# Raw key products kept in memory for the second half of a two-direction delta rule

## The chip, the cores and the metric

The kernel runs on one core of a Trainium2 chip. The metric is device time in microseconds (us) for one execution. The core has five instruction streams that run in order and meet only through semaphores: TensorE (PE in the profile; PEld is its weight load), VectorE (DVE), ScalarE (ACT), GpSimd (POOL) and SyncE (SP), which here issues DMAs.

## The reference, cut to what matters

The whole is one layer of an encoder: a projection, two mixers side by side, an output projection and a mixture of experts. The change lies in one of the mixers, a gated delta rule over 1024 tokens with 4 heads of 128, run forward and backward over the same keys, queries and values and summed:

```python
decay = where(tril, exp(g_i - g_j), 0)                 # g: cumulative log-decay, one per direction
a_mat = where(strict, einsum('id,jd->ij', k * beta, k) * decay, 0)
attn  = where(tril,   einsum('id,jd->ij', q, k) * decay, 0)
...
o_f = gated_delta_chunked(q, k, v, g[:, 0], beta[:, 0])
o_b = flip(gated_delta_chunked(flip(q), flip(k), flip(v), flip(g[:, 1]), flip(beta[:, 1])))
```

Per chunk `a_mat` (its system is inverted) and `attn` start from two raw products, keys by keys and keys by queries. These raw products don't depend on the direction; beta, decay and the mask do.

## The kernel before, in words

The function `delta_net` holds both directions, d = 0 and d = 1. A chunk is 128 tokens, so there are TT = 8 steps t; direction 0 takes chunk t in step t and direction 1 takes chunk 7 - t. Over the first four steps the two directions thus cover all eight chunks, and in the last four each meets the chunks that the other has already had.

There is one order of work, written out by hand in `delta_schedule` as a list of names with a step; every engine walks that same list and picks out the names it serves, for d = 0 and then d = 1. An engine never runs ahead of its own order. One round of the list (the loop variable t) mixes work of four steps: it starts with `z4` of step t and ends with `d6` of t; `read_k`, `read_q`, `solve`, `attend`, `new_state` belong to step t - 1, `kq` to t + 1 and `kk` to t + 2. Names that the prediction uses:

- `kk`: PE multiplies the keys of a chunk by themselves, 4 heads into the PSUM bank `O[d]`. DVE then makes `amat` of it (L1037): four `scalar_tensor_tensor` of 128x128, product times -beta times decay.
- `kq`: PE multiplies keys by queries into bank `V[d]`; DVE multiplies the bank by the masked decay into `attn` (L1046), one `tensor_tensor` of 128x512.
- `z4`, `d4`, `turn4`, `z5`, `d5`, `turn5`, `z6`, `d6`: the inverse of a chunk's system, built by doubling blocks. `z4` needs the 16-wide diagonal inverses spread out in memory by POOL (`spread_tt`, `spread_t`, L1150) and the masked level of `amat` (`alev4`, `alev5`, L1144, POOL). After `d4`, DVE adds (L1051) and PE transposes the sum (`turn4`, L936).
- `base`: DVE inverts the 16x16 diagonal blocks in small instructions (L996 to L1020), between the add of `d4` and that of `d5`.
- `read_k`: PE, keys by state; DVE makes the residual `resid` of it (L1061). `attend`: PE; when it is done POOL may write the next `mask` (L1157). `new_state`: PE, then DVE updates the state (L1075).
- `add_o`: only in steps 4 to 7, POOL adds an output to the sum (L1177).

POOL's order within a round is `alev4`, `vb` (L1163), `mask`, `alev5`, from step 4 on `add_o`, `spread_tt`, `spread_t`, two instructions of each (d = 0, 1). SP's queue stores `amat`, loads its diagonal blocks back, stores the inverses and loads them as `T_cols`.

A line with an "L910" is any product of the helper `heads`: it stands for all matmuls of 4 heads, told apart by their tiles. One such product for both directions shows as x16.

Of the kernel before, what the change touches and what calls it, by code (L numbers as in the profile page):

```python
# [26 lines left out]
ALU = mybir.AluOpType  # L27
ACT = mybir.ActivationFunctionType
AX = mybir.AxisListType

P = 128
# [3 lines left out]
TT = L // P  # L35
H = 4
# [738 lines left out]
def delta_net(nc, core, c, a, out, tb, o_sum, a_dram, x_dram, g_dram):  # L775
# [6 lines left out]
    qT, kT, kv = out["qT"], out["kT"], out["kv"]  # L782

    def buf(name, n=1):
        return [core.sb(f"{name}{d}", [P, n, H, P]) for d in range(2)]

    e_b, ab_b, as_b, at_b, tt_b = buf("decay", 2), buf("amat", 2), buf("alev", 2), buf("attn", 2), buf("TT", 2)
# [7 lines left out]
    inv_t = core.sb("blocks_inv_t", [NB, 256])  # L795
    prod = core.sb("blocks_prod", [NB, 512])
    half = core.sb("blocks_half", [NB, 64])
    X = [core.ps(f"bank_x{d}", [P, H, P]) for d in range(2)]
    Y = [core.ps(f"bank_y{d}", [P, H, P]) for d in range(2)]
    V = [core.ps(f"bank_v{d}", [P, H, P]) for d in range(2)]  # L800
    O = [core.ps(f"bank_o{d}", [P, H, P]) for d in range(2)]
    names = ("kk kq absd decay masked amat attn alev t16 tt16 z zc dd tt t tt6 ks r solved vn vdec vb qs o_part "
             "av kv o o_added state a_out blk_ld tc_ld t_out").split()
    S = {n: [core.sem(f"dn_{n}{d}") for d in range(2)] for n in names}
    gb_ld = [[core.sem(f"dn_gb_ld{d}{s}") for s in range(2)] for d in range(2)]
    based, base_step, x_out = core.sem("dn_based"), core.sem("dn_base_step"), core.sem("dn_x_out")
# [1 line left out]
    def chunk(t, d):  # L808
        return t if d == 0 else TT - 1 - t
# [23 lines left out]
    def late(d):  # L833
        return HALF[1 - d]
# [7 lines left out]
    with nc.Block() as block:  # L842
# [59 lines left out]
        @block.tensor  # L902
        def _(pe):
            def wait(name, d, n):
                if n > 0:
                    pe.wait_ge(S[name][d], n)

            def heads(dst, lhs, rhs):
                for h in range(H):
                    mm = pe.matmul(dst[:, h, :], lhs(h), rhs(h), start=True, stop=True)  # L910
                return mm

            for name, t, d in delta_schedule():
                cs, b = cols(t, d), t % 2
                if name == "kk":
                    wait("state", d, t - 1)
                    wait("amat", d, t)
                    heads(O[d], lambda h: kT[:, h, cs], lambda h: kT[:, h, cs]).then_inc(S["kk"][d], 1)
                elif name == "kq":
                    wait("attn", d, t)  # L920
                    wait("o", d, t - 1)
                    heads(V[d], lambda h: kT[:, h, cs], lambda h: qT[:, h, cs]).then_inc(S["kq"][d], 1)
                elif name == "z4":
                    wait("zc", d, 3 * t)
                    wait("alev", d, 2 * t + 1)
                    wait("tt16", d, t + 1)
                    heads(X[d], lambda h: as_b[d][:, 0, h, :], lambda h: tt16_b[d][:, 0, h, :]).then_inc(S["z"][d], 1)
                elif name == "d4":
                    wait("zc", d, 3 * t + 1)
                    wait("tt6", d, t)  # L930
                    wait("t16", d, t + 1)
                    heads(Y[d], lambda h: t16_b[d][:, 0, h, :], lambda h: z_b[d][:, 0, h, :]).then_inc(S["dd"][d], 1)
                elif name in ("turn4", "turn5"):
                    wait("tt", d, 2 * t + (1 if name == "turn4" else 2))
                    for h in range(H):
                        mm = pe.transpose(X[d][:, h, :], tt_b[d][:, b, h, :], c["ident"][:])  # L936
                    mm.then_inc(S["t"][d], 1)
                elif name == "z5":
                    wait("alev", d, 2 * t + 2)
                    wait("t_out", d, 2 * t + 1)  # L940
                    heads(X[d], lambda h: as_b[d][:, 1, h, :], lambda h: tt_b[d][:, b, h, :]).then_inc(S["z"][d], 1)
                elif name == "d5":
                    wait("zc", d, 3 * t + 2)
                    heads(Y[d], lambda h: t_b[d][:, 0, h, :], lambda h: z_b[d][:, 0, h, :]).then_inc(S["dd"][d], 1)
                elif name == "z6":
                    wait("t_out", d, 2 * t + 2)
                    wait("amat", d, t + 1)
                    lo, up = late(d), early(d)
                    for h in range(H):
                        mm = pe.matmul(X[d][up, h, 0:64], ab_b[d][lo, b, h, up], tt_b[d][lo, b, h, lo],  # L950
                                       start=True, stop=True)
                    mm.then_inc(S["z"][d], 1)
                elif name == "d6":
                    wait("zc", d, 3 * t + 3)
                    up = early(d)
                    for h in range(H):
                        mm = pe.matmul(Y[d][up, h, 0:64], t_b[d][up, 0, h, up], z_b[d][up, 0, h, 0:64],
                                       start=True, stop=True)
                    mm.then_inc(S["dd"][d], 1)
                elif name == "read_k":  # L960
                    wait("state", d, t + 1)
                    wait("attn", d, min(t + 2, TT))
                    wait("o", d, t)
                    heads(V[d], lambda h: kT[:, h, cs], lambda h: s_b[d][:, 0, h, :]).then_inc(S["ks"][d], 1)
                elif name == "read_q":
                    wait("amat", d, min(t + 3, TT))
                    heads(O[d], lambda h: qT[:, h, cs], lambda h: s_b[d][:, 0, h, :]).then_inc(S["qs"][d], 1)
                elif name == "solve":
                    wait("tt6", d, t + 1)
                    wait("r", d, t + 1)  # L970
                    heads(V[d], lambda h: tt_b[d][:, b, h, :], lambda h: r_b[d][:, 0, h, :]).then_inc(S["solved"][d], 1)
                elif name == "attend":
                    wait("vdec", d, t + 1)
                    wait("vn", d, t + 1)
                    heads(V[d], lambda h: at_b[d][:, b, h, :], lambda h: vn_b[d][:, 0, h, :]).then_inc(S["av"][d], 1)
                elif name == "new_state":
                    wait("o_part", d, t + 1)
                    heads(O[d], lambda h: rows(0, t, d)[:, h, :], lambda h: vd_b[d][:, 0, h, :]
                          ).then_inc(S["kv"][d], 1)

        @block.vector
        def _(dve):
            def wait(name, d, n):
                if n > 0:
                    dve.wait_ge(S[name][d], n)
# [42 lines left out]
            for name, t, d in delta_schedule():  # L1028
                ch, b = chunk(t, d), t % 2
                if name == "kk":  # L1030
                    wait("kk", d, t + 1)
                    wait("decay", d, t + 1)
                    wait("z", d, 3 * (t - 1))
                    wait("alev", d, 2 * (t - 1))
                    wait("a_out", d, 16 * (t - 1))
                    for h in range(H):
                        ins = dve.scalar_tensor_tensor(out=ab_b[d][:, b, h, :], in0=O[d][:, h, :],  # L1037
                                                       scalar=head_col("nbeta", t, d, h), in1=e_b[d][:, b, h, :],
                                                       op0=ALU.mult, op1=ALU.mult)
                    ins.then_inc(S["amat"][d], 1)  # L1040
                elif name == "base":
                    invert_blocks(t)
                elif name == "kq":
                    wait("kq", d, t + 1)
                    wait("masked", d, t + 1)
                    dve.tensor_tensor(at_b[d][:, b], V[d][:], at_b[d][:, b], ALU.mult).then_inc(S["attn"][d], 1)  # L1046
                elif name == "d4":
                    wait("dd", d, 3 * t + 1)
                    wait("tt16", d, t + 1)
# [6 lines left out]
                elif name == "read_k":  # L1056
# [3 lines left out]
                    for h in range(H):  # L1060
                        ins = dve.scalar_tensor_tensor(out=r_b[d][:, 0, h, :], in0=V[d][:, h, :],  # L1061
                                                       scalar=head_col("nbetaG", t, d, h), in1=vb_b[d][:, 0, h, :],
                                                       op0=ALU.mult, op1=ALU.add)
# [7 lines left out]
                elif name == "new_state":  # L1071
                    wait("kv", d, t + 1)
                    wait("state", d, t + 1)
                    for h in range(H):
                        ins = dve.scalar_tensor_tensor(out=s_b[d][:, 0, h, :], in0=s_b[d][:, 0, h, :],  # L1075
                                                       scalar=head_col("eTot", t, d, h), in1=O[d][:, h, :],
                                                       op0=ALU.mult, op1=ALU.add)
# [3 lines left out]
        def _(act):  # L1081
            def wait(name, d, n):
                if n > 0:
                    act.wait_ge(S[name][d], n)

            for name, t, d in delta_schedule():
                b, up = t % 2, early(d)
                if name == "decay":
# [4 lines left out]
                    ins.then_inc(S["absd"][d], 1)  # L1093
                    wait("absd", d, t + 1)
                    act.activation(e_b[d][:, b], e_b[d][:, b], ACT.Exp, scale=-1.0).then_inc(S["decay"][d], 1)
                elif name in ("z4", "z5"):
                    n = 3 * t + (1 if name == "z4" else 2)
                    wait("z", d, n)
# [1749 lines left out]
```

## Time and profile before

| what | us |
|---|---|
| median of 3 runs (lowest, highest) | 1543.13 (1542.45, 1543.61) |
| the profiled execution's own time | 1542.74 |
| its span, first to last instruction | 1541.0 |
| delta rule's stretch in the span | about 321 to 560 |
| PE busy over the span | 1321.7 (86%) |
| DVE, ACT, POOL busy over the span | 1086.2, 828.5, 397.1 |

The rows further down are read from one profiled execution. Each timeline row gives start, duration, engine, line, operation, the tiles (output<-inputs), the shape and a count; in brackets the idle time of the engine before it and what ended it. Rows with a count above 1 are merged neighbours.

### The profile page before, as it was taken

The numbers are of one execution on the slowest core, as the hardware profiler recorded it, in microseconds if no ns is written. First come the engines' busy times: TensorE is split into PE (matmuls) and PEld (weight loads), VectorE is DVE, ScalarE is ACT, GpSimd is POOL, SyncE is SP. The second block draws the span as 40 slices with busy tenths as digits, with TensorE's granted clock in tenths as the row PEclk, the third lists the DMA queues.
The fourth block names the chain that finished last, engine by engine and source line by source line (L and its number), as shares of the span: only waits on it lengthen the run. The fifth ranks groups of instructions, "written<-read, shape, count | busy, mean of one in ns | idle before, by whom it ended". The sixth has DMA issues, their size and how long they took to land. (4 is left out here: it accounts for less than half of the span.)

```text
span 1541.0 us, 23093 instructions
## 1 busy us (share of the span) xinstructions
PE 1321.7 (86%) x7750; PEld 1130.7 (73%) x7750; DVE 1086.2 (70%) x1339; ACT 828.5 (54%) x1025; POOL 397.1 (26%) x378
## 2 busy tenths in 40 slices
PE   4999999936999958787994589999999999999930
PEld 4999887836999957645883478888888888888820
DVE  5884886654777568904225588888888888888818
ACT  7563444432656450034221377777787778787712
POOL 5110220015565645702210011211111221111113
PEclk9999999967999978998996599999999999999975
DMA  8264976012221137721113399999999999999727
GB/s 250 90 212 151 302 222 179 9 57 52 49 67 46 22 150 276 271 110 32 42 42 123 138 366 399 421 409 411 408 408 410 412 413 412 407 406 413 319 93 291
DMA packets 149680, 357.85 MB, mean 232 GB/s; under 512 B 41999, under 2 KB 94443, under 8 KB 122475
## 3 DMA queue, kind: packets, MB, share of 16 engines
q1 hardware_dynamic: 131803, 297.12, 51.5%
q0 software_dynamic: 11904, 40.42, 7.9%
q10 hardware_dynamic: 5904, 19.40, 3.1%
q8 instruction: 42, 0.69, 0.2%
q14 instruction: 27, 0.22, 0.0%
HBM read 287.62 MB, written 69.27 MB: 232 GB/s over the span
## 5 line engine op out<-in xcount | busy, mean ns | idle before, releaser
L2647 DVE TENSOR_TENSOR w_lo<-w_down,w_hi 128x2048 fp32r<-128x2048 f32 x66 | 148.4, 2288 | 65.7 <-ACT w_hi L2588 65.7
L2647 DVE TENSOR_TENSOR w_lo<-w_gate,w_hi 128x2048 fp32r<-128x2048 f32 x66 | 149.6, 2287 | 15.3 <-ACT w_hi L2588 15.3
L2588 ACT ACTIVATE w_hi<-w_up 128x2048 fp32r<-128x2048 f32 x66 | 126.7, 1923 | 49.9 <-PE down_mm L2541 49.9
L2647 DVE TENSOR_TENSOR w_lo<-w_up,w_hi 128x2048 fp32r<-128x2048 f32 x66 | 150.5, 2286 | 3.8 <-ACT w_hi L2588 0.2
L2479 POOL COPY gather_idx<-slot_token 128x1 int32 (+1 forms) x34 | 26.6, 781 | 486.0 <-PE x_turned L2503 453.5
L2588 ACT ACTIVATE w_hi<-w_down 128x2048 fp32r<-128x2048 f32 x66 | 123.4, 1914 | 45.8 <-issue 22.7
L2588 ACT ACTIVATE w_hi<-w_gate 128x2048 fp32r<-128x2048 f32 x66 | 126.8, 1923 | 30.3 <-PE up_mm L2515 29.5
L2513 PE MATMUL gate_mm<-w_hi,gathered_T_hi 128*128 128x512 f32 x264 | 107.5, 407 | 10.6 <-DVE w_lo L2647 5.3
L2539 PE MATMUL down_mm<-w_hi,hidden_T_hi 128*128 128x512 f32 x264 | 106.8, 404 | 9.0 <-DVE hidden_T_lo L2681 9.0
L2513 PE MATMUL up_mm<-w_hi,gathered_T_hi 128*128 128x512 f32 x264 | 105.9, 401 | 0.0
L2514 PE MATMUL gate_mm<-w_lo,gathered_T_hi 128*128 128x512 f32 x264 | 105.1, 398 | 0.0
L2515 PE MATMUL gate_mm<-w_hi,gathered_T_lo 128*128 128x512 f32 x264 | 104.9, 397 | 0.0
L2540 PE MATMUL down_mm<-w_lo,hidden_T_hi 128*128 128x512 f32 x264 | 103.9, 394 | 0.0
L2541 PE MATMUL down_mm<-w_hi,hidden_T_lo 128*128 128x512 f32 x264 | 103.8, 393 | 0.0
L2515 PE MATMUL up_mm<-w_hi,gathered_T_lo 128*128 128x512 f32 x264 | 103.3, 391 | 0.0
L2514 PE MATMUL up_mm<-w_lo,gathered_T_hi 128*128 128x512 f32 x264 | 102.8, 389 | 0.0
L2482 POOL DMA_INDIRECT gathered<-h_rows,gather_idx x34 | 81.9, 2410 | 26.9 <-POOL gather_idx L2479 26.9
L283 PE MATMUL proj_ps<-hT_hi,w_split 128*128 128x512 f32 x192 | 77.4, 403 | 0.0
L284 PE MATMUL proj_ps<-hT_lo,w_split 128*128 128x512 f32 x192 | 75.9, 395 | 0.0
L285 PE MATMUL proj_ps<-hT_hi,w_split 128*128 128x512 f32 x192 | 75.9, 395 | 0.0
L2513 PEld LDWEIGHTS gate_mm<-w_hi,gathered_T_hi 128*128 128x128 f32 x264 | 50.9, 193 | 28.0 <-issue 18.1
L2539 PEld LDWEIGHTS down_mm<-w_hi,hidden_T_hi 128*128 128x128 f32 x264 | 50.2, 190 | 18.7 <-DVE w_lo L2647 9.1
(430 smaller groups left out, 3359.9 us busy)
## 6 DMA issues: line engine op xcount, KB each, us to landing
w_down<-in_expert_w_down SPq DMA_DIRECT2D x66, 1024.0 KB, 6.9
w_gate<-in_expert_w_gate SPq DMA_DIRECT2D x64, 1024.0 KB, 7.6
w_up<-in_expert_w_up SPq DMA_DIRECT2D x64, 1024.0 KB, 8.3
expert_rows_dram<-expert_out ACTq DMA_DIRECT2D x33, 512.0 KB, 8.5
expert_rows_dram<-ones SPq DMA_DIRECT2D x32, 512.0 KB, 6.3
s_rows<-s_rows_dram SPq DMA_DIRECT2D x9, 1184.0 KB, 6.1
x<-s_rows_dram SPq DMA_DIRECT2D x7, 1184.0 KB, 5.2
w_raw<-in_w_in SPq DMA_DIRECT2D x12, 512.0 KB, 6.0
```

Of the source, the lines that this page charges most:

```text
L283: pe.matmul(dst, left(0), right(0), start=k == 0, stop=False)
L284: pe.matmul(dst, left(0), right(1), start=False, stop=False)
L285: return pe.matmul(dst, left(1), right(0), start=False, stop=k == KT - 1)
L2482: pool.indirect_dma_start(out=xg[:, s, :], out_offset=None, in_=h_dram, in_offset=bass.IndirectOffsetOnAxis(ap=idx[:, s:s + 1], axis=0)).t ...
L2513: pe.matmul(dst, xT_hi[:, k, :], hi[:, at, cols], start=k == 0, stop=False)
L2514: pe.matmul(dst, xT_hi[:, k, :], lo[:, at, cols], start=False, stop=False)
L2515: mm = pe.matmul(dst, xT_lo[:, k, :], hi[:, at, cols], start=False, stop=k == KT - 1)
L2539: pe.matmul(dst, hT_hi[:, k, :], hi[:, at, cols], start=k == 0, stop=False)
L2540: pe.matmul(dst, hT_hi[:, k, :], lo[:, at, cols], start=False, stop=False)
L2541: mm = pe.matmul(dst, hT_lo[:, k, :], hi[:, at, cols], start=False, stop=k == KD - 1)
L2588: act.activation(hi[:, slot(s, j), :], flat(j), ACT.Copy).then_inc(S["piece_hi"], 1)
L2647: dve.tensor_tensor(lo[:, at, :], flat(j), hi[:, at, :].bitcast(F32), ALU.subtract).then_inc(S["piece_lo"], 1)
```

## The change

Two buffers in SBUF, `k_keys` and `k_queries`, hold the raw products of all eight chunks. In steps 0 to 3 the PE makes the products as before, DVE uses them from PSUM as before, and ACT then copies the banks to the buffers, 16 copies in all; the PE's next use of the bank also waits for the copy. In steps 4 to 7 the PE makes neither product, and DVE reads the other direction's copy from SBUF.

```diff
+    k_keys = core.sb("keys_by_keys", [P, TT, H, P])
+    k_queries = core.sb("keys_by_queries", [P, TT, H, P])
+    SHARED = TT // 2
@@ PE
-                if name == "kk":
+                if name == "kk" and t < SHARED:
                     wait("state", d, t - 1)
                     wait("amat", d, t)
+                    wait("kept_kk", d, t)
                     heads(O[d], ...kT..., ...kT...).then_inc(S["kk"][d], 1)
-                elif name == "kq":
+                elif name == "kq" and t < SHARED:
                     wait("attn", d, t)
+                    wait("kept_kq", d, t)
                     wait("o", d, t - 1)
                     heads(V[d], ...kT..., ...qT...).then_inc(S["kq"][d], 1)
                 elif name == "read_k":
                     wait("state", d, t + 1)
-                    wait("attn", d, min(t + 2, TT))
+                    wait("attn", d, min(t + 2, SHARED))
+                    wait("kept_kq", d, min(t + 2, SHARED))
                 elif name == "read_q":
-                    wait("amat", d, min(t + 3, TT))
+                    wait("amat", d, min(t + 3, SHARED))
+                    wait("kept_kk", d, min(t + 3, SHARED))
@@ DVE
                 if name == "kk":
-                    wait("kk", d, t + 1)
+                    if t < SHARED:
+                        wait("kk", d, t + 1)
+                    else:
+                        wait("kept_kk", 1 - d, TT - t)
+                    gram = O[d] if t < SHARED else k_keys[:, ch]
                     ...
-                        ins = dve.scalar_tensor_tensor(..., in0=O[d][:, h, :],
+                        ins = dve.scalar_tensor_tensor(..., in0=gram[:, h, :],
                                   scalar=head_col("nbeta", t, d, h), in1=e_b[d][:, b, h, :],
                 elif name == "kq":
-                    wait("kq", d, t + 1)
+                    if t < SHARED:
+                        wait("kq", d, t + 1)
+                    else:
+                        wait("kept_kq", 1 - d, TT - t)
+                    gram = V[d][:] if t < SHARED else k_queries[:, ch]
                     wait("masked", d, t + 1)
-                    dve.tensor_tensor(at_b[d][:, b], V[d][:], at_b[d][:, b], ALU.mult)
+                    dve.tensor_tensor(at_b[d][:, b], gram, at_b[d][:, b], ALU.mult)
@@ ACT
+                elif name == "kk" and t < SHARED:
+                    wait("amat", d, t + 1)
+                    act.activation(k_keys[:, chunk(t, d)], O[d][:], ACT.Copy).then_inc(S["kept_kk"][d], 1)
+                elif name == "kq" and t < SHARED:
+                    wait("attn", d, t + 1)
+                    act.activation(k_queries[:, chunk(t, d)], V[d][:], ACT.Copy).then_inc(S["kept_kq"][d], 1)
```

## Rows read from the trace of the kernel before

**Rows 1.** One round by windows: length, busy us of each engine, granted clock, DMA

```profile
472.10:496.45 24.35, 24.16 (x225) 23.32 (x224) 18.05 (x54) 14.53 (x40) 14.45 (x13) 1.00 0.20 55
```

**Rows 2.** Timeline around z4 of step 5, PE

```profile
473.15 2.05 PE L910 MATMUL bank_o<-kT 128*128 128x128 f32 x16
...
475.04 1.95 PE L910 MATMUL bank_v<-qT,kT 128*128 128x128 f32 x16
...
477.81 2.05 PE L910 MATMUL bank_x<-TT,alev 128*128 128x128 f32 x16
...
483.60 1.27 PE L936 MATMUL bank_x<-ident,TT 128*128 128x128 f32 x8 [0.17 <-DVE TT L1051]
```

**Rows 3.** Timeline of the same stretch, DVE

```profile
471.26 2.16 DVE L1075 SCALAR_TENSOR_TENSOR state<-state,tab_eTot,bank_o 128x128 f32<-128x128 f32 x8 [1.08 <-PE bank_o L910]
474.35 2.16 DVE L1037 SCALAR_TENSOR_TENSOR amat<-bank_o,tab_nbeta,decay 128x128 f32<-128x128 f32 x8 [0.93 <-PE bank_o L910]
476.42 1.29 DVE L1046 TENSOR_TENSOR attn<-bank_v,attn 128x512 f32<-128x512 f32 x2
480.79 2.16 DVE L1061 SCALAR_TENSOR_TENSOR resid<-bank_v,tab_nbetaG,vb 128x128 f32<-128x128 f32 x8 [3.08 <-PE bank_v L910]
482.87 1.29 DVE L1051 TENSOR_TENSOR TT<-TT,bank_y 128x512 f32<-128x512 f32 x2
```

**Rows 4.** Timeline of the same stretch, POOL

```profile
468.71 1.28 POOL L1157 TENSOR_TENSOR attn<-decay,upto_f 128x512 f32<-128x512 f32 x1 [8.99 <-PE bank_v L910]
...
473.64 2.50 POOL L1150 TENSOR_TENSOR TT<-T_cols,diag 128x512 f32<-128x512 f32 x2
...
479.11 1.27 POOL L1144 TENSOR_TENSOR alev<-amat,level_f 128x512 f32<-128x512 f32 x1 [0.53 <-PE bank_x L910]
```

**Rows 5.** Timeline of a later round, POOL's add_o and PE's z4 of step 7

```profile
522.32 2.51 POOL L1177 TENSOR_TENSOR o_sum<-o_sum,otmp 128x512 f32<-128x512 f32 x2
...
526.20 3.26 PE L910 MATMUL bank_x<-TT,alev 128*128 128x128 f32 x16 [1.61 <-POOL TT L1150]
```

**Rows 6.** All instructions of two DVE lines: ns min/median/max, first and last start

```profile
L1046 DVE TENSOR_TENSOR attn<-bank_v,attn x16: 677/690/692, 336.7 to 523.7; 128x512 f32<-128x512 f32 x16
...
L1007 DVE TENSOR_TENSOR blocks_prod<-blocks_inv,blocks x8: 682/684/685, 342.2 to 513.3; 64x512 f32<-64x512 f32 x8
```

**Rows 7.** Timeline of the same small DVE instruction, beside POOL and alone

```profile
360.61 1.26 POOL L1157 TENSOR_TENSOR attn<-decay,upto_f 128x512 f32<-128x512 f32 x1
360.88 1.01 DVE L1000 TENSOR_TENSOR blocks_prod<-blocks_inv,blocks 64x8 f32<-64x8 f32 x1
...
387.57 0.16 DVE L1000 TENSOR_TENSOR blocks_prod<-blocks_inv,blocks 64x8 f32<-64x8 f32 x1
```

**Rows 8.** Timeline of a later stage, two neighbouring DVE instructions beside POOL

```profile
643.49 0.61 DVE L1870 TENSOR_TENSOR s_z<-s_rot 128x256 f32<-128x256 f32 x1
643.77 0.91 POOL L1903 TENSOR_TENSOR s_back<-s_scanned,s_rows 128x254 f32<-128x254 f32 x1
644.02 0.95 DVE L1871 TENSOR_TENSOR s_z<-s_rot 128x256 f32<-128x256 f32 x1
```

**Rows 9.** All instructions of a DVE line in the stage after this one

```profile
L1982 DVE TENSOR_TENSOR silu_z<-silu_z,gn_rs x8: 678/1752/1758, 568.8 to 578.6; 128x512 f32<-128x512 f32 x8
```

**Rows 10.** Windows after PE stood idle; the number behind POOL's is the clock

```profile
375.00:377.00 2.00, 2.00 (x11) 2.00 (x11) 0.23 (x1) 0.14 (x1) 1.01 (x1) 0.51 0.49 49
...
527.00:529.00 2.00, 1.94 (x10) 1.75 (x10) 0.00 (x0) 0.60 (x1) 2.00 (x3) 0.54 0.00 0
...
530.00:531.00 1.00, 1.00 (x8) 1.00 (x8) 0.01 (x1) 0.09 (x1) 0.00 (x0) 0.71 0.00 0
```

**Rows 11.** Timeline, ACT before and in z4 of step 5

```profile
477.63 0.78 ACT L1115 ACTIVATE TT<-bank_y 64x256 f32<-64x256 f32 x2 [4.00 <-PE bank_y L957]
479.00 0.60 ACT L1100 ACTIVATE zc<-bank_x 128x512 f32<-128x512 f32 x1 [0.60 <-PE bank_x L910]
```

**Rows 12.** Timeline, DVE in the first round and PE after its longest later idle time

```profile
337.95 0.69 DVE L1046 TENSOR_TENSOR attn<-bank_v,attn 128x512 f32<-128x512 f32 x1 [0.54 <-POOL attn L1157]
...
371.18 1.97 PE L936 MATMUL bank_x<-ident,TT 128*128 128x128 f32 x8 [7.75 <-DVE TT L1055]
```

More of the change, by code:

```diff
@@ L802, in delta_net @@
     names = ("kk kq absd decay masked amat attn alev t16 tt16 z zc dd tt t tt6 ks r solved vn vdec vb qs o_part "
-             "av kv o o_added state a_out blk_ld tc_ld t_out").split()
+             "av kv o o_added state a_out blk_ld tc_ld t_out kept_kk kept_kq").split()
     S = {n: [core.sem(f"dn_{n}{d}") for d in range(2)] for n in names}
@@ L1036, in _ @@
                     for h in range(H):
-                        ins = dve.scalar_tensor_tensor(out=ab_b[d][:, b, h, :], in0=O[d][:, h, :],
+                        ins = dve.scalar_tensor_tensor(out=ab_b[d][:, b, h, :], in0=gram[:, h, :],
                                                        scalar=head_col("nbeta", t, d, h), in1=e_b[d][:, b, h, :],
@@ L1043, in _ @@
                 elif name == "kq":
-                    wait("kq", d, t + 1)
+                    if t < SHARED:
[3 more added lines that the diff above has]
+                    gram = V[d][:] if t < SHARED else k_queries[:, ch]
                     wait("masked", d, t + 1)
-                    dve.tensor_tensor(at_b[d][:, b], V[d][:], at_b[d][:, b], ALU.mult).then_inc(S["attn"][d], 1)
+                    dve.tensor_tensor(at_b[d][:, b], gram, at_b[d][:, b], ALU.mult).then_inc(S["attn"][d], 1)
                 elif name == "d4":
```

## Prediction

> **What bounds the kernel now.** First the page, for the delta rule's stretch of the span; then windows cut at the starts of successive z4 products. In a steady round PE is busy 24.16 of 24.35 us at full clock, DVE 18.05, ACT 14.53, POOL 14.45 [rows 1]. So PE's issue sets the round, and taking work from PE shortens it until the next thing is late. The timelines of PE, DVE and POOL over one round show what that is. I count from the start Z of a round's z4; the next z4 comes at Z+24.35 (477.81 in [rows 2]), and rows just ahead of it are placed backward from there. turn4 starts at Z+5.79, the DVE add behind d4 having let it go [rows 2]. POOL's mask starts at Z+15.25, let go by attend, and with its neighbours forms a row of queued POOL instructions 1.23 apart: mask, alev5, spread_tt from Z+20.18, spread_t until Z+25.1 [rows 4]. DVE ends the state update at Z+19.96, then does amat, attn, waits 3.08 us, then does the residual and the add that turn4 wants [rows 3]. DVE has 3 us to spare there, and POOL's spread_tt for direction 0 is ready at Z+21.45, 2.9 us ahead of need. Once, before step 7, PE came early enough to meet it: there POOL has add_o to do too, and z4 waited 1.61 us [rows 5].
>
> **Removed from PE.** A product pair costs 475.04 - 473.15 = 1.89 us of issue [rows 2]; kk goes for steps 4 to 7 and kq for steps 4 to 7, eight pairs, 15 us. Of those PE can't cash all. Between z4(2) and z4(3) only kk(4) is gone: -1.9. In a round where both are gone PE would be ready at Z+20.6, but spread_tt ends at Z+21.45: -2.9 at most, -2.6 when the second direction's spread, 1.23 behind where PE wants it 0.9 behind, is counted. In the rounds with add_o (two more POOL instructions, 2.46) it ends at Z+23.9: -0.4, then nothing, for there z4 waits already [rows 5]. Without any new cost: 1.9 + 2.6 + 2.6 + 0.4 = 7.5 us.
>
> **Added to ACT.** Sixteen copies of 128x512 out of PSUM, 0.60 each [rows 11]. Per round that is 2.4 us, in the 4.00 us that ACT stands idle ahead of the d6 copy [rows 11]; the banks are next written by read_k and read_q, the first of them 1.9 us after z4 starts, the copies of attn being done by then. Cost 0. In the first round that idle time isn't there: the decays of step 1 now stand behind two copies that wait for amat of step 0, and kk(1) behind a copy. Bounds: 0, since attn of direction 1 already waits 0.54 us for POOL [rows 12], and 1.9, two copies plus the 0.7 us or so of waiting for amat; I take 0.2, because base(0) stands behind that attn on DVE and POOL's mask isn't moved.
>
> **Changed on DVE, and this is what decides.** In steps 4 to 7 amat (4 instructions a direction) and attn (1) read both tensors from SBUF instead of one from PSUM. By themselves they cost the same: a 512-column instruction with both inputs in SBUF took 684 ns, attn with one in PSUM 690 [rows 6]. The Trainium skill, VectorE: DVE Perf Modes, section on the TRN2 errata, gives SBUF sources 58 fixed cycles against 120 for PSUM; by that table each of some 10 instructions a round would be about 65 ns shorter, an estimate of 0.65 us a round. The rows show 6 ns, so I add nothing.
>
> But such an instruction can't run beside POOL. A product of 64x8 elements from two SBUF tensors took 0.16 us alone and 1.01 us when issued at 360.88, 0.27 behind a POOL instruction; it ended at 361.89, POOL's at 361.87 [rows 7]. It waited for the whole POOL instruction. Two neighbours on DVE without a wait between them show what a queue of them does: the first ended at 644.10, the second, issued at 644.02, at 644.97, which is 0.29 behind the end of the POOL instruction that began at 643.77 [rows 8]. So POOL gets in between two queued DVE instructions: one passes per POOL instruction. The 128x512 ones took 1752 ns beside POOL against 678 [rows 9]. All of these are tensor_tensor; that scalar_tensor_tensor behaves alike is my step. The Trainium skill, SBUF — State Buffer, section Who interferes with whom, says it of any DVE instruction with two SBUF inputs against a GpSimd instruction that reads SBUF, and that the loser blocks fully.
>
> Now one late round. The amat of both directions, 8 instructions, start at Z+19.96, with POOL's row in full flow. They pass at its ends: Z+20.2, 21.45, 22.7, 23.95, 25.2 (the spreads), 26.45 (alev4 of direction 0). alev4 of direction 1 waits for amat itself, so the last two pass freely until Z+27.1; two attn at 0.65 give Z+28.3, or 29.3 if the second meets alev4. Queued behind them on DVE are the residual (2.08) and the add for turn4 (0.69): turn4 can start at Z+31.1 to 32.1. z4 had started at Z+21.45 = Z', so turn4 starts at Z'+9.7 to 10.7 instead of Z'+5.79, and PE stands idle 3.9 to 4.9 us. From turn4 on nothing shortens: 9.46 to mask, 6.2 to the end of spread_tt. The round is 25.3 to 26.3, against 24.35 before; with add_o 27.8 to 28.8, against 24.35 and 24.05. Rounds 3 to 6 pay: 2 x (1.0 to 2.0) + 3.5 to 4.5 + 3.8 to 4.8 = 9.3 to 13.3, less 1.9 for the round before: +7.4 to +11.4, middle +9.4.
>
> **The clock.** After 1.61 us of idle PE ran at 0.5 of the clock (1.2 GHz) until about 530.5, from 527 on [rows 10]; after 7.75 us of idle it ran at half speed from 371.18 until about 377 [rows 12, 10]. The first cost 1.7 us (half of 3.5), the second 2.9 (half of 5.8). The stalls ahead of turn4 lie between, and what follows them (read_q to attend) is packed and leads to the mask. Four stalls at 2.3: +9.2; bounds 4 x 1.7 = 6.8 and 11.6, and 0 if the clock holds.
>
> **Sum.** 9.4 + 9.2 + 0.2 = +18.8 us. The profiled execution took 1542.74 (span 1541.0, 1.7 around it), so 1561.5; it lies 0.4 under the median of the runs, which makes 1562. Behind the delta rule nothing changes: every engine waits for its end.
>
> **Rivals.** A difference under 0.2% (3.1 us) I count as none.
>
> - *The port is shared without loss* (ends faster). If scalar_tensor_tensor isn't held up, or the attn alone is, the 7.5 us stand, less one more clock dip (1.7) in the first add_o round, where PE now waits some 3 us for POOL: -5.8, 1537. For it: no row shows that instruction form blocked. Against: rows 7 to 9. It decides from the point where DVE is free by Z+24.4. Chance 0.14.
> - *DVE keeps the port through its own queue.* Then POOL waits once, for a run of 8 amat and 2 attn (3.4 us), and spread_tt ends at about Z+24.9 without add_o, Z+27.3 with it: rounds of -0.8, +0.5, +0.5, +3, +1.2, together +4.4, and up to two dips more, so 1547 to 1551. Against it: rows 8, where POOL got in between. Chance 0.10.
> - *No change in sum*: gain and loss cancel, because POOL's row has gaps where I see it full. 1541 to 1546. Chance 0.06.
> - *The forecast*: chance 0.70, 1550 (clock holds) to 1568 (upper bounds, with the start's 1.9 instead of 0.2), likeliest 1562.
>
> **How the numbers follow.** Range 1547 to 1571: nearly all of the forecast's case, 3 us above it because the DMA chain from amat (store, blocks back, base) loses some 5 us of slack and may add to it, and most of the second rival: about 0.79. Faster 0.15 (first rival, a little of the third), same 0.05, slower 0.80.
>
> **What would show it.** Right: in rounds 3 to 6 the L1037 instructions that read keys_by_keys take about 1.3 us each instead of 0.34 while POOL works; turn4's wait for the L1051 add grows from 0.17 to 4 or 5 us; z4 to z4 is 22.5, then over 25; windows behind turn4 show clocks near 0.5. Right on the rest: ACT's copies at 0.60 with no PE wait on them in rounds 1 to 3, z4(1) where it was within a microsecond. Wrong: L1037 at 0.34 beside POOL means the first rival; POOL instructions of 2 us or more with unmoved DVE means the second. If L1037 is held up but turn4 isn't late, my slack was misread.

## The result, and the profile after

| | before | after |
|---|---|---|
| median of the runs, us | 1543.37 (1542.45 to 1543.95, 4 runs) | 1560.79 (1559.94 to 1562.77, 4 runs) |
| profiled execution, us | 1542.74, span 1541.0 | 1562.77, span 1561.0 |
| mean granted clock | 0.926 | 0.917 |

The changed kernel is slower: ratio 1.0115, 95% interval 1.0098 to 1.0133, that is 17.4 us by the medians. The profiled execution is the slowest of its four. 2.5 us of its length arose ahead of the delta rule, whose first product starts at 323.95 after against 321.42 before.

Starts of z4 by step, read from PE's timeline, and the distances between them:

| z4 of step | 0 | 1 | 2 | 3 | 4 | 5 | 6 | 7 |
|---|---|---|---|---|---|---|---|---|
| before | 352.54 | 380.42 | 404.76 | 429.11 | 453.46 | 477.81 | 502.15 | 526.20 |
| after | 354.32 | 383.03 | 407.39 | 429.96 | 458.51 | 486.27 | 517.96 | 547.15 |
| distance before | | 27.88 | 24.34 | 24.35 | 24.35 | 24.35 | 24.34 | 24.05 |
| distance after | | 28.71 | 24.36 | 22.57 | 28.55 | 27.76 | 31.69 | 29.19 |

From z4(1) to z4(7) it is 145.78 before and 164.12 after, +18.3 us: one round shorter by 1.8, then four longer by 4.2, 3.4, 7.3 and 5.1.

Lines of the changed file are higher by 3 to 21: amat L1037 is L1048, attn L1046 is L1061, the add behind d4 L1051 is L1066, the spreads L1150 are L1171, alev L1144 is L1165, PE's products L910 and L936 are L913 and L941.

The groups of instructions of amat, with the two sources kept apart; the numbers behind the count are ns, shortest, median, longest:

```profile
L1048 DVE SCALAR_TENSOR_TENSOR amat<-bank_o,tab_nbeta,decay x32: 341/343/352, 330.4 to 405.7; 128x128 f32<-128x128 f32 x32
L1048 DVE SCALAR_TENSOR_TENSOR amat<-keys_by_keys,tab_nbeta,decay x32: 339/1343/1361, 427.3 to 521.7; 128x128 f32<-128x128 f32 x32
```

The same instruction on the same number of elements takes 343 ns out of PSUM and, in the median, 1343 out of SBUF; its shortest out of SBUF is 339, so the source by itself costs nothing. The timeline of a late round shows who is beside it. DVE, which answers to [rows 3]:

```profile
482.42 2.16 DVE L1090 SCALAR_TENSOR_TENSOR state<-state,tab_eTot,bank_o 128x128 f32<-128x128 f32 x8 [1.08 <-PE bank_o L913]
484.49 7.41 DVE L1048 SCALAR_TENSOR_TENSOR amat<-keys_by_keys,tab_nbeta,decay 128x128 f32<-128x128 f32 x8
491.82 2.35 DVE L1061 TENSOR_TENSOR attn<-keys_by_queries,attn 128x512 f32<-128x512 f32 x2
494.09 2.15 DVE L1076 SCALAR_TENSOR_TENSOR resid<-bank_v,tab_nbetaG,vb 128x128 f32<-128x128 f32 x8
496.16 1.27 DVE L1066 TENSOR_TENSOR TT<-TT,bank_y 128x512 f32<-128x512 f32 x2
```

POOL in the same stretch, which answers to [rows 4]:

```profile
484.82 2.58 POOL L1171 TENSOR_TENSOR TT<-T_cols,diag 128x512 f32<-128x512 f32 x2
487.36 2.60 POOL L1171 TENSOR_TENSOR T<-T_cols,diag 128x512 f32<-128x512 f32 x2
489.91 1.31 POOL L1165 TENSOR_TENSOR alev<-amat,level_f 128x512 f32<-128x512 f32 x1
491.98 1.65 POOL L1165 TENSOR_TENSOR alev<-amat,level_b 128x512 f32<-128x512 f32 x1 [0.75 <-DVE amat L1048]
```

Eight amat took 7.41 us instead of 2.16. POOL has five instructions between 484.82 and 491.22, and five of the eight amat lie beside them at 1.35 us each. The first took 0.52, and the last two, while POOL itself waits 0.75 us for amat, pass freely at 0.34. DVE had 3.08 us of idle time ahead of resid before [rows 3]; now it has none and comes late. What PE waited for:

```profile
436.13 3.75 PE L913 MATMUL bank_v<-state,kT 128*128 128x128 f32 x16 [4.12 <-ACT keys_by_queries L1116]
...
458.51 3.65 PE L913 MATMUL bank_x<-TT,alev 128*128 128x128 f32 x16 [0.73 <-POOL TT L1171]
...
469.11 1.97 PE L941 MATMUL bank_x<-ident,TT 128*128 128x128 f32 x8 [3.38 <-DVE TT L1066]
...
486.27 2.40 PE L913 MATMUL bank_x<-TT,alev 128*128 128x128 f32 x16 [0.74 <-POOL TT L1171]
...
496.89 1.97 PE L941 MATMUL bank_x<-ident,TT 128*128 128x128 f32 x8 [4.64 <-DVE TT L1066]
...
517.96 3.75 PE L913 MATMUL bank_x<-TT,alev 128*128 128x128 f32 x16 [3.26 <-POOL TT L1171]
...
528.03 1.26 PE L941 MATMUL bank_x<-ident,TT 128*128 128x128 f32 x8 [1.88 <-DVE TT L1066]
...
547.15 3.73 PE L913 MATMUL bank_x<-TT,alev 128*128 128x128 f32 x16 [4.12 <-POOL TT L1171]
```

In three late rounds turn4 waits 3.38, 4.64 and 1.88 us for the add, where it waited 0.17 [rows 2]. In the first one (from 429.96) the wait is elsewhere: PE stands at read_k of step 2, which follows z4 of step 3, until ACT has copied the last raw product away. The duration of the group behind a wait shows the clock: 16 products of z4 take 2.05 to 2.4 us at full clock and 3.65 to 3.75 at half, 8 of turn4 1.27 and 1.97. Windows, the four late rounds first (length, busy us of PE, PEld, DVE, ACT and POOL, granted clock, DMA), then PE alone behind waits:

```profile
429.96:458.51 28.55, 23.36 (x194) 22.45 (x193) 22.50 (x53) 16.28 (x44) 13.76 (x13) 0.88 0.20 50
458.51:486.27 27.76, 23.54 (x192) 22.92 (x193) 24.24 (x54) 14.55 (x40) 15.06 (x13) 0.88 0.20 51
486.27:517.96 31.69, 23.55 (x192) 22.77 (x193) 26.75 (x56) 14.77 (x40) 17.59 (x15) 0.87 0.17 44
517.96:547.15 29.19, 23.01 (x193) 22.28 (x193) 24.40 (x51) 11.08 (x30) 18.33 (x15) 0.85 0.14 31
...
436.00:438.00 2.00, 1.87 (x9) 0.50 0.35 60
...
470.00:472.00 2.00, 2.00 (x12) 0.50 0.53 186
...
498.00:500.00 2.00, 2.00 (x12) 0.50 0.19 71
```

PE was busy 24.16 of 24.35 us before [rows 1]. It has 3.8 us less to do, which leaves 20.4, and yet it is busy 23.0 to 23.6: some 3 us a round are what the products at half clock (1.2 GHz) took longer.

### The profile page after: what moved, and what is told of

It reads as the page before. It is cut to its first block and busy times, and to the rows that moved or that the text cites. A ratio compares the mean times of both kernels' runs of the same rounds, so it can differ in the third digit from the quotient of the medians.

```text
span 1561.0 us, 22871 instructions
## 1 busy us (share of the span) xinstructions
PE 1319.7 (85%) x7622; PEld 1130.2 (72%) x7622; DVE 1112.2 (71%) x1339; ACT 838.1 (54%) x1041; POOL 399.8 (26%) x378
```

## The experiments

Each ratio is to the kernel before, run on the same chip with that group: e1 to e4, e5 to e8, e9 and e10. Between groups, ratios compare better than microseconds.

**e1: the copies alone.** PE makes every product and DVE reads PSUM; ACT still copies sixteen banks to SBUF, and nothing reads them.

```diff
-                if name == "kk" and t < SHARED:
+                if name == "kk":
-                    gram = O[d] if t < SHARED else k_keys[:, ch]
+                    gram = O[d]
-                    gram = V[d][:] if t < SHARED else k_queries[:, ch]
+                    gram = V[d][:]
```

> PE makes all products as before and DVE reads them from PSUM; ACT only adds its 16 copies in steps 0 to 3 and PE waits for them. Theory (the loss is VectorE's two-SBUF-input instructions held up by POOL): the copies fit into ACT's idle time, so within 0.5 us of before, about 1543. Rival (the new waits on the kept copies cost): several us over before, seen as PE waits on keys_by_keys or keys_by_queries in rounds 1 to 3.

1543.1 us, ratio 0.9995 (0.9985 to 1.0004); the rounds from z4(1) on are 24.35 and 24.04, those of before. The copies are there at the duration assumed:

```profile
L1107 ACT ACTIVATE keys_by_keys<-bank_o x8: 579/597/597, 329.6 to 403.7; 128x512 f32<-128x512 f32 x8
```

ACT's 9.6 us are hidden: from the first product to z4(1) it is 59.00 us (321.57 to 380.57), as before the change.

**e2: DVE reads SBUF, but PE still makes all products.** The late products are made and used by nobody; amat and attn of the late steps read the kept copies.

```diff
-                if name == "kk" and t < SHARED:
+                if name == "kk":
-                elif name == "kq" and t < SHARED:
+                elif name == "kq":
```

> PE makes all products in all eight steps, though those of steps 4 to 7 are used by nobody; DVE reads the copies from SBUF in steps 4 to 7. Theory: the amat still take about 1.3 us each beside POOL; DVE is free at about Z+28.9, turn4 at Z+31.9, against a z4 at Z+24.35, so 1.7 us late, and the rounds with add_o somewhat more: 7 to 14 us over before, 1550 to 1557. Rival (a pure PE effect, such as shorter rounds running into POOL's spreads): the time of before, 1543.

1559.18 us, ratio 1.0108 (1.0093 to 1.0124): 15.8 us slower than before, 2 above the expected range. The late rounds are 27.01, 26.53, 26.53 and 31.23. Two of PE's waits, by its timeline:

```profile
466.42 1.25 PE L941 MATMUL bank_x<-ident,TT 128*128 128x128 f32 x8 [2.35 <-DVE TT L1066]
...
521.42 1.97 PE L941 MATMUL bank_x<-ident,TT 128*128 128x128 f32 x8 [4.11 <-DVE TT L1066]
```

So the source that DVE reads makes the loss, whatever PE saves. Set beside the changed kernel at 1560.79, whose PE has 15 us less to issue, it is no slower (ratios 1.0108 and 1.0115, inside each other's interval): the work taken away bought nothing once DVE was late. What lies over my range sits in the last round, 7.2 us over its 24.05, with a fall of the clock (8 products of turn4 in 1.97 us).

**e3: ACT copies the products back into the PSUM banks.** PE makes no late product, as in the change, but DVE reads both operands as it did before.

```diff
-                    gram = O[d] if t < SHARED else k_keys[:, ch]
+                        wait("back_kk", d, t + 1 - SHARED)
+                    gram = O[d]
...
+                elif name == "kk":
+                    wait("kept_kk", 1 - d, TT - t)
+                    wait("state", d, t - 1)
+                    wait("amat", d, t)
+                    act.activation(O[d][:], k_keys[:, chunk(t, d)], ACT.Copy).then_inc(S["back_kk"][d], 1)
```

and the same for kq and the V banks.

> As the changed kernel, but in steps 4 to 7 ACT copies the kept products from SBUF back into the PSUM banks and DVE reads them there, with one SBUF input as before. PE's savings stay, ACT does 16 copies more of about 0.6 us. Theory: no DVE instruction is held up, amat back at 0.34 us each, and the 7.5 us that PE saves show, less one clock dip in a round with add_o: 1536 to 1539. Rival (the loss comes from the saved PE time itself, or from the kept buffers and waits): near the changed kernel, 1555 or more. Rival (ACT's copies come too late): 1543 to 1550, DVE waiting for bank_o from ACT.

1540.58 us, ratio 0.9986 (0.9977 to 0.9996). The 17.4 us are gone, and amat is at 343 ns again in every step. But the gain over before is 2.8 us, under the 4 to 7 that I expected. The rounds are 22.56, 21.59, 23.71, 25.70 and 26.69: the first two are as the prediction has them for a change without hold-up, and then z4 meets POOL. PE's timeline and windows of PE behind those waits:

```profile
449.98 3.33 PE L913 MATMUL bank_x<-TT,alev 128*128 128x128 f32 x16 [0.69 <-POOL TT L1181]
...
473.69 3.28 PE L913 MATMUL bank_x<-TT,alev 128*128 128x128 f32 x16 [1.21 <-POOL TT L1181]
...
526.08 3.39 PE L913 MATMUL bank_x<-TT,alev 128*128 128x128 f32 x16 [3.21 <-POOL TT L1181]
```

```profile
474.00:476.00 2.00, 2.00 (x13) 0.59 0.68 260
500.00:502.00 2.00, 2.00 (x11) 0.50 0.24 23
```

**e4: the change, with PE's idle time filled.** Eighteen groups of products that nobody uses, ahead of read_k of step 2, turn4 of steps 4 and 5, and z4 of steps 6 and 7; otherwise the changed kernel.

```diff
+                n = {("read_k", 2): 4, ("turn4", 4): 3, ("turn4", 5): 4, ("z4", 6): 3, ("z4", 7): 4}.get((name, t), 0)
+                if n and d == 0:
+                    for i in range(2):
+                        wait("state", i, t + 1 if name == "read_k" else t)
+                    for i in range(n):
+                        heads(O[i % 2], lambda h: kT[:, h, cs], lambda h: kT[:, h, cs])
```

> The changed kernel with unused 128x128 products (18 groups of four heads in all, 0.9 us each at full clock) put on PE where it stood idle: ahead of read_k of round 3, turn4 of rounds 4 and 5, z4 of steps 6 and 7. Nothing else changes. Theory of the clock (four stalls at about 2.3 us each of half speed behind them): the granted clock stays near 1.00 through rounds 3 to 6, and the kernel is 5 to 9 us faster than the changed one, 1552 to 1556. Rival (the half clock lies beside other work and costs nothing): no change, 1561, or slower by what the products overrun.

1554.48 us, ratio 1.0080 (1.0064 to 1.0095): with more work on PE it is 6.3 us faster than the changed kernel by the medians, 5.4 by the ratios to before. Two waits of turn4:

```profile
465.32 1.25 PE L947 MATMUL bank_x<-ident,TT 128*128 128x128 f32 x8 [1.97 <-DVE TT L1072]
...
520.27 1.97 PE L947 MATMUL bank_x<-ident,TT 128*128 128x128 f32 x8 [4.12 <-DVE TT L1072]
```

The clock stayed up at the first (8 products in 1.25 us), and fell at the second, the one in front of which nothing was put. The clock's part of the loss is therefore some 6 us and one fall more. What is left, some 9 to 12 us, is the hold-up itself; this is a difference of times and was not measured by itself.

**e5: fewer products kept.** Keys by keys of steps 1 to 3 only, copied back into PSUM for steps 4 to 6; PE makes everything else.

```diff
-                if name == "kk" and t < SHARED:
+                if name == "kk" and (t < SHARED or t == TT - 1):
...
-                elif name == "kq" and t < SHARED:
+                elif name == "kq":
```

> keys by keys kept for steps 1 to 3 only, and copied back by ACT into the PSUM bank for steps 4 to 6; PE makes the products of step 7 and all keys by queries again. No DVE operation reads both inputs from SBUF. Theory (a round can be shortened only as far as POOL's row is ready, and each time PE meets POOL ahead of z4 its clock falls to half): three rounds lose 1.9 us each and come at about 22.5, z4 waits for POOL nowhere but before step 7 (as before the change), so about 1537 to 1539, under e3's 1540.6 though PE does ten more product pairs (19 us) less than half of which e3 could cash. Rival (POOL is met anyway, or ACT's copies come late): rounds over 22.5 with a wait of z4 or d4, 1540 to 1544.

1537.54 us, ratio 0.9961 (0.9948 to 0.9974), inside the expected range and faster than e3 although PE makes ten more of the 16 product groups that e3 leaves out. Three rounds are 22.57, 22.57, 22.57, the next 24.37 and 24.04. It leaves out six groups at 0.94 us [rows 2], 5.7 us, and the three rounds return 5.3 of it, for PE never meets POOL ahead of z4 in them. (The expectation counts ten more product pairs and 19 us for PE; it is ten groups, five pairs, 9.4 us.)

**e6: e3 with its idle time filled.** Unused products ahead of z4 of step 5 (one group) and of steps 6 and 7 (three each).

```diff
+                n = {4: 0, 5: 1, 6: 3, 7: 3}.get(t, 0)
+                if name == "z4" and n and d == 0:
+                    for i in range(2):
+                        wait("zc", i, 3 * t)
+                    for i in range(n):
+                        heads(X[i % 2], lambda h: kT[:, h, cs], lambda h: kT[:, h, cs])
```

> e3 with unused products (1 group of 4 ahead of z4 of step 5, 3 groups ahead of steps 6 and 7) in the time in which PE waited for POOL. Theory (e3's gain was eaten by half-clock stretches behind these waits): the granted clock stays near 1.0 from step 4 on and the time falls 2 to 4 us under e3's 1540.6, to about 1537. Rival (e3 was short because of POOL's pace alone): no change or slower by the products' own time, 1540 to 1543.

1536.01 us, ratio 0.9955 (0.9944 to 0.9967). Windows of PE at the place where e3 has 0.50:

```profile
500.00:502.00 2.00, 1.91 (x17) 1.00 0.17 15
502.00:504.00 2.00, 2.00 (x20) 1.00 0.19 17
```

The rounds are 22.57, 21.60, 23.45, 24.37 and 24.32. Useless work on PE made e3 faster by about 0.3%, 4.6 us by the medians where 2 to 4 were expected, so what ate its gain was the clock behind the waits for POOL. One fall is left: ahead of z4 of step 4 nothing was put, PE waits 0.70 us there, and its 16 products take 3.27 us.

**e7: only keys by queries kept.** PE makes keys by keys in every step and amat reads PSUM; attn of the late steps reads SBUF.

```diff
-                    gram = O[d] if t < SHARED else k_keys[:, ch]
+                    gram = O[d]
```

> only keys by queries are kept and read from SBUF; PE makes keys by keys in every step, amat reads PSUM. Theory (each DVE instruction with two SBUF inputs is held up by one POOL instruction): two held-up attn instead of ten instructions a round, some 1.3 us later at most, against 3 us of room on DVE; POOL's row grows by some 0.4 us a held-up neighbour; PE saves 1.87 a round. amat from SBUF is absent, amat stays at 343 ns, no wait of 4 us ahead of turn4. About 1541 to 1546, within 0.2% of before. Rival (the attn does as much harm as amat, or the kept copies do): above 1550.

1541.69 us, ratio 0.9996 (0.9984 to 1.0007), no difference that can be told. The groups of attn show that it is held up too:

```profile
L1056 DVE TENSOR_TENSOR attn<-bank_v,attn x8: 679/692/692, 336.9 to 428.0; 128x512 f32<-128x512 f32 x8
L1056 DVE TENSOR_TENSOR attn<-keys_by_queries,attn x8: 906/1609/1750, 451.8 to 520.3; 128x512 f32<-128x512 f32 x8
```

and the timeline of DVE that two held-up instructions fit into the room that DVE had:

```profile
451.77 3.15 DVE L1056 TENSOR_TENSOR attn<-keys_by_queries,attn 128x512 f32<-128x512 f32 x2
454.84 2.15 DVE L1071 SCALAR_TENSOR_TENSOR resid<-bank_v,tab_nbetaG,vb 128x128 f32<-128x128 f32 x8
```

turn4 waits 0.64 us there.

**e8: one amat instruction a direction.** ACT multiplies by -beta while it copies keys by keys to SBUF, four copies with a scale instead of one. The late amat is then one tensor_tensor of 128x512 where the change has four scalar_tensor_tensor of 128x128, over the same elements.

```diff
+                    if t >= SHARED:
+                        dve.tensor_tensor(ab_b[d][:, b], gram, e_b[d][:, b], ALU.mult).then_inc(S["amat"][d], 1)
+                        continue
...
+                    for h in range(H):
+                        ins = act.activation(k_keys[:, chunk(t, d), h, :], O[d][:, h, :], ACT.Copy,
+                                             scale=head_col("nbeta", TT - 1 - t, 1 - d, h))
```

> the change, but ACT folds -beta into the kept key products (four copies with a scale instead of one), so that the late amat is one tensor_tensor of 128x512 a direction: 2 DVE instructions where the change has 8, over the same elements. Theory (one queued DVE instruction passes for each POOL instruction, so that the count of instructions sets the delay): amat and attn are 4 held-up instructions, DVE is free some 2 us a round earlier than after the change, and the stall of turn4 falls from 4 to about 2 or less: 1553 to 1556. Rival (the delay goes by the elements read, a shared bandwidth): the two amat take as long together as the eight (7.4 us) and the time stays at 1561.

1546.47 us, ratio 1.0015 (1.0002 to 1.0027). The sign of the expectation held, its size did not: 14 us less than the changed kernel where I expected 5 to 8. Groups of amat, and then the timelines of DVE (a round without add_o, then one with it), of POOL and of PE in the latter:

```profile
L1048 DVE TENSOR_TENSOR amat<-keys_by_keys,decay x8: 679/908/1748, 424.9 to 497.5; 128x512 f32<-128x512 f32 x8
```

```profile
470.50 1.51 DVE L1048 TENSOR_TENSOR amat<-keys_by_keys,decay 128x512 f32<-128x512 f32 x2
471.94 2.34 DVE L1064 TENSOR_TENSOR attn<-keys_by_queries,attn 128x512 f32<-128x512 f32 x2
...
496.63 2.58 DVE L1048 TENSOR_TENSOR amat<-keys_by_keys,decay 128x512 f32<-128x512 f32 x2
499.13 3.41 DVE L1064 TENSOR_TENSOR attn<-keys_by_queries,attn 128x512 f32<-128x512 f32 x2
...
496.95 3.38 POOL L1204 TENSOR_TENSOR o_sum<-o_sum,otmp 128x512 f32<-128x512 f32 x2
500.29 3.37 POOL L1177 TENSOR_TENSOR TT<-T_cols,diag 128x512 f32<-128x512 f32 x2
503.61 2.47 POOL L1177 TENSOR_TENSOR T<-T_cols,diag 128x512 f32<-128x512 f32 x2
...
502.13 3.75 PE L913 MATMUL bank_x<-TT,alev 128*128 128x128 f32 x16 [4.46 <-POOL TT L1177]
...
510.35 1.27 PE L941 MATMUL bank_x<-ident,TT 128*128 128x128 f32 x8 [0.17 <-DVE TT L1069]
```

The eight amat of the changed kernel in the round that this one with add_o answers to:

```profile
513.67 9.37 DVE L1048 SCALAR_TENSOR_TENSOR amat<-keys_by_keys,tab_nbeta,decay 128x128 f32<-128x128 f32 x8
```

With POOL's row full, two amat take 2.58 us where eight took 9.37 over the same elements: the price goes by instructions. In the round before it amat and attn are done 3.8 us after amat began (470.50 to 474.28), against 9.7 after the change (484.49 to 494.17). DVE is early again and turn4 waits 0.17 us as before the change; I had left it 2 us of its wait, and that is, as far as the trace tells, the gain beyond the expected one. What is left comes from the other side: beside a 128x512 DVE instruction with two SBUF inputs a POOL instruction takes 1.70 us (3.38 for two) instead of 1.25 (2.47 for two). Four of them make POOL's row 1.8 us longer, and z4 waits 4.46 us for it.

**e9: before, with one gap filled.** The kernel before the change, with one group of unused products ahead of z4 of step 7, where it waited 1.61 us [rows 5].

```diff
+                if name == "z4" and t == TT - 1 and d == 0:
+                    for i in range(2):
+                        wait("zc", i, 3 * t)
+                    heads(X[0], lambda h: kT[:, h, cs], lambda h: kT[:, h, cs])
```

> the kernel before the change with one group of unused products (128x512 out, into bank_x of direction 0) ahead of z4 of step 7, where PE waited 1.61 us for POOL and ran at half clock for 3.5 us behind it. Theory (the clock falls behind such a gap, price 1.7 us as in the prediction): z4(7) stays within 0.3 us of 526.20, the windows behind it show a clock near 1.0, the end of the delta rule comes some 1.5 us earlier: 1542 against 1543.4, at the edge of what times can tell, so read from the trace. Rival (the clock falls for another reason): windows at half clock stay, the time is the same or 0.3 longer.

1541.12 us, ratio 0.9985 (0.9976 to 0.9994). PE's timeline:

```profile
527.37 2.34 PE L910 MATMUL bank_x<-TT,alev 128*128 128x128 f32 x16 [0.54 <-POOL TT L1154]
...
533.45 1.27 PE L940 MATMUL bank_x<-ident,TT 128*128 128x128 f32 x8 [0.17 <-DVE TT L1055]
```

From z4(7) to its turn4 it is 6.08 us, against 7.60 before (526.20 to 533.80): the fall of the clock had cost 1.5 us, the prediction's 1.7 within 0.2. z4(7) itself comes 24.05 us behind z4(6), as before. By the ratio the kernel gained 2.3 us (0.9 to 3.7); the trace accounts for 1.5 of them.

**e10: e5 with the same gap filled.** The four lines of e9 in e5.

> e5 with the same group of unused products ahead of z4 of step 7. Theory: e5's rounds stay at 22.57 three times, the dip behind z4(7) goes, 1.5 us under e5: about 1536. Rival: as e5, 1537.5.

1536.56 us, ratio 0.9956 (0.9942 to 0.9969), not to be told from e5. The trace says why nothing could be won: in e5's profiled execution the clock had not fallen behind that wait at all. PE's timeline of e5:

```profile
521.53 2.34 PE L913 MATMUL bank_x<-TT,alev 128*128 128x128 f32 x16 [1.63 <-POOL TT L1170]
```

Sixteen products in 2.34 us after 1.63 us of idle, where before it was 3.26 us after 1.61 [rows 5]. So a gap of this length does not bring a fall each time. For that reason e9's trace alone can't tell whether the filling kept the clock up or a fall happened not to come; that the filling did it rests on e9's times, whose interval leaves out 1.

e5, e6 and e10 beat both kernels, by 0.4 to 0.45% of before, and can't be told apart.

## Why the prediction was right, point by point

**The sum.** +18.8 us were forecast. The medians show +17.4; the median 1560.79 lies 1.2 under the forecast. The two profiled executions are 20.0 apart: 18.3 in the rounds, 0.1 in the start, 2.5 ahead of the delta rule, and 0.9 given back behind z4(7). The nearness of 18.3 and 18.8 is in part luck: below, two terms are off on opposite sides and one stall stands in another place than forecast.

**Removed from PE.** -1.9 between z4(2) and z4(3): -1.78. Right.

**ACT's copies.** 0 for sixteen of them, 0.2 for the start. e1 showed no cost, and from the first product to z4(1) it is 59.08 us after, 59.00 before. The changed kernel's wait of PE on a copy, which the prediction did not have, is told below.

**The held-up instructions.** The mechanism was as the prediction put it, also for scalar_tensor_tensor, which was its open step: 1343 ns against 343, where about 1.3 us was forecast. turn4 was to start at Z'+9.7 to 10.7 and started at 10.60, 10.62 and 10.07. PE's wait ahead of it was to be 3.9 to 4.9 us and was 3.38, 4.64 and 1.88; the two short ones lie behind a z4 at half clock, which filled part of the time. In the add_o round the last two amat were held up too (9.37 us for the eight), where the prediction let them pass freely in every round. e3 takes nothing away but the second SBUF operand and the loss is gone; e8 keeps the operand and cuts the count of instructions, and most of the loss is gone. That one queued instruction passes for each POOL instruction is seen in the 7.41 and 9.37 us of the changed kernel and in the 2.58 of e8. The Trainium skill, SBUF — State Buffer, section Who interferes with whom, makes the shared ports an exclusive lock; the 7.41 us for eight instructions that take 2.16 alone agree with it, and the alternation of two queues is what the trace adds. The Trainium skill's table in VectorE: DVE Perf Modes, section on the TRN2 errata, would have made the instruction some 65 ns shorter out of SBUF, an estimate from its 58 and 120 fixed cycles; its shortest was 339 ns against 341 out of PSUM, so no such gain is seen, as the prediction had assumed.

**By rounds.** Hold-up and clock together were to cost rounds 3 and 4 3.3 to 4.3 us each, and the two with add_o 5.8 to 6.8 and 6.1 to 7.1. Measured: 4.2, 3.4, 7.3 and 5.1. The last two are outside, on opposite sides, and partly cancel. Behind turn4 of step 5 two more things came late than I had counted, the fall of the clock and POOL's wait for it; behind turn4 of step 6, after 1.88 us of idle, the clock did not fall (8 products in 1.26 us).

**Where round 3 stalls was wrong.** I had the stall of every late round at turn4. In the first one it is at read_k, 4.12 us. attn of step 3 still reads PSUM, and is queued on DVE behind amat of step 4, the first that is held up:

```profile
427.26 7.38 DVE L1048 SCALAR_TENSOR_TENSOR amat<-keys_by_keys,tab_nbeta,decay 128x128 f32<-128x128 f32 x8
434.56 1.28 DVE L1061 TENSOR_TENSOR attn<-bank_v,attn 128x512 f32<-128x512 f32 x2
```

read_k needs attn's bank, and the bank's copy by ACT stands between them. The step that failed is the sentence on ACT that the banks are next written with "the copies of attn being done by then": worked out with DVE as it was before, and not again with the DVE that the next part made late. The price was the same by luck: 4.12 us at read_k instead of 4 to 5 at turn4.

**The clock.** Four falls at 2.3 us, for the stalls ahead of turn4, were forecast. There were six, at read_k, at two of the turn4 and at three of the z4 (one of these, ahead of step 7, the kernel before has too); some lay ahead of a wait for DVE that would have come anyway and cost nothing. Filling the gaps gave back 6.3 us with one fall left (e4); the 9.2 were of the right size, put in partly wrong places.

**The first rival** was the one on the other side, and e3 is the kernel that it describes. It was to give 1537 and gave 1540.6. Its term for the clock, one fall, was too small. e3 met POOL in four rounds, at 0.69, 1.21, 3.14 and 3.21 us, and ran at half clock behind each. With the last three gaps filled (e6) it gave 7.5 us; 1.5 of these are the fall before step 7's turn4 that the kernel before has too (e9). That leaves 6 us, with one fall still in it: from z4(4) to its turn4 e6 takes 7.40 us, against 6.10 a step later, 1.3 more. The gain without new cost was thus some 7 us where the prediction had 7.5; by the rounds of the two traces it is 6.4 (145.78 less 140.67 from z4(1) to z4(7), and the 1.3).

**The second rival** is out: POOL's spreads were let in between DVE's instructions. POOL did pay a little, 0.04 us beside a 128x128 instruction (2.58 for two against 2.50 [rows 4]) and 0.4 beside attn.

**Left open.** What decides whether the clock falls behind a gap of 0.7 to 2 us was not settled: 1.61 us in before did it, 1.63 in e5 and 1.88 after the change did not; and of two waits of the changed kernel for spread_tt, z4 of step 4 ran at half clock behind 0.73 us and z4 of step 5 at full clock behind 0.74. The places and number of falls in a forecast like this one are therefore open. How e8's 14 us divide between DVE's earlier end and the clock was not tried with its gaps filled.

## What to carry to other kernels

When an operand moves from PSUM to SBUF, ask whether the instruction now has two SBUF inputs, what GpSimd does at that time, and how many such instructions stand in a row: here each waited for one GpSimd instruction, so count them, not their elements, and give the engine's idle time ahead of the next consumer as the budget. Work taken from the engine that sets the pace is worth no more than the lead of the next engine, and past that point it can cost, since here the gap often halved TensorE's clock; here 5.7 us of removed issue (e5) gave more than 15 (e3). A copy by an idle ScalarE back into PSUM was a cheap way to keep the operand where it did no harm.

## What the runs showed of the hardware that was not expected

- GpSimd is held up as well, by the length of what DVE does: its 128x512 instruction takes 1.27 us alone, 1.31 beside 128x128 instructions of DVE with two SBUF inputs (the changed kernel), and 1.70 beside 128x512 ones (e8). The kernel before showed this already in its next stage: beside the instructions of [rows 9] POOL's took 1.71 to 1.72 us, from 569.12 to 577.54. Fewer and longer DVE instructions moved part of the cost from DVE to GpSimd in e8.
- TensorE ran at half clock behind waits as short as 0.69 us (e3, z4 of step 4: 16 products in 3.33 us) and at full clock behind one of 1.88 us (after, turn4 of step 6) and of 1.63 us (e5).
- Products that nobody uses made three kernels faster: the changed one by 6.3 us, e3 by 0.3% and the kernel before by 0.15% (0.06 to 0.24), in each case with full clock behind the filled gaps, where it had been half.
